# Twelve runs of unread products in the instruction stream of the matrix engine of a two-block transformer kernel

## The reference

```
# first model, layers 0 and 1
m = hybrid_mixer(x) if i == 0 else mla_mixer(x)     # recurrent + top-k attention; latent attention
h = layer_norm(ALPHA * x + m)
f = square(relu(h @ mlp_w1)) @ mlp_w2               # 1024 -> 4096 -> 1024
e = sigmoid(h @ ple_w_gate) * (p @ ple_w_proj)
x = layer_norm(ALPHA * h + f + e)
# second model, layers 0 and 1, on latent (512) and context (256) tokens
h = modulate(rms_norm(x), ...)                      # then ab_mixer (mLSTM + windowed attention) or c_mixer
x = x + gate * mixer(h)
x = x + gate * (square(relu(modulate(rms_norm(x)) @ w1)) @ w2)
```

## Time and profile before

| | us |
|---|---|
| three executions | 3631.1, 3635.57, 3611.84 (median 3631.1) |
| profiled execution, its own time | 3620.35 |
| span of its instructions | 3618.6 |
| PE busy | 3330.8 (92%) |
| PE weight loads busy | 2592.0 (72%) |
| DVE busy | 1654.2 (46%) |
| ACT busy | 1220.9 (34%) |
| POOL busy | 82.8 (2%) |
| mean granted clock of PE | 0.924 |

### The profile page before, as it was taken

How to read it: one execution, slowest core, us unless ns; L and a number is a source line. 1 busy time by engine, 2 the same in 40 slices (tenths; PEclk the granted TensorE clock), 3 DMA queues, 4 the chain that set the end, 5 groups by cost and what they waited for, 6 DMA issues and landing times. The chain is left out here.

```text
span 3618.6 us, 40069 instructions
## 1 busy us (share of the span) xinstructions
PE 3330.8 (92%) x15236; PEld 2592.0 (72%) x15236; DVE 1654.2 (46%) x2745; ACT 1220.9 (34%) x2016; POOL 82.8 (2%) x88
## 2 busy tenths in 40 slices
PE   7899999999999999999985998899999988989999
PEld 6576677763576677767864876778888865767777
DVE  3753566651253566653235565332332334343334
ACT  2343233322463233334121333232222233543332
POOL 4000000000000000000000010000000000000000
PEclk9859999999999999998985785999999989999999
DMA  4201434422301433421210000111111111012221
GB/s 153 71 1 53 150 130 155 162 96 35 82 1 53 169 133 134 162 81 47 62 50 1 1 1 1 47 47 70 52 64 70 46 47 47 1 47 93 93 93 70
DMA packets 160797, 259.40 MB, mean 72 GB/s; under 512 B 58476, under 2 KB 73194, under 8 KB 160556
## 3 DMA queue, kind: packets, MB, share of 16 engines
q1 hardware_dynamic: 158932, 252.94, 19.8%
q10 hardware_dynamic: 1628, 4.76, 0.3%
q0 software_dynamic: 128, 0.26, 0.0%
HBM read 255.85 MB, written 2.10 MB: 71 GB/s over the span
## 5 line engine op out<-in xcount | busy, mean ns | idle before, releaser
L1104 ACT ACTIVATE w_hi<-wbuf 128x1024 fp32r<-128x1024 f32 x330 | 348.9, 1060 | 1324.7 <-PE psA L726 1275.2
L724 PE MATMUL psA<-act_hi,w_hi 128*128 128x512 f32 (+1 forms) x1824 | 699.7, 384 | 62.6 <-DVE act_lo L1682 43.1
L725 PE MATMUL psA<-act_lo,w_hi 128*128 128x512 f32 (+1 forms) x1824 | 684.6, 375 | 0.0
L726 PE MATMUL psA<-act_hi,w_lo 128*128 128x512 f32 (+1 forms) x1824 | 683.9, 375 | 0.0
L1676 DVE TENSOR_TENSOR w_lo<-wbuf,w_hi 128x1024 fp32r<-128x1024 f32 x330 | 404.0, 1227 | 562.7 <-ACT w_hi L1104 555.1
L724 PE MATMUL psA<-hid_hi,w_hi 128*128 128x512 f32 (+1 forms) x1280 | 480.3, 375 | 34.3 <-ACT work L1104 30.9
L725 PE MATMUL psA<-hid_lo,w_hi 128*128 128x512 f32 (+1 forms) x1280 | 472.0, 369 | 0.0
L726 PE MATMUL psA<-hid_hi,w_lo 128*128 128x512 f32 (+1 forms) x1280 | 471.7, 369 | 0.0
L724 PEld LDWEIGHTS psA<-act_hi,w_hi 128*128 128x128 f32 x1824 | 349.8, 192 | 148.1 <-issue 52.6
L725 PEld LDWEIGHTS psA<-act_lo,w_hi 128*128 128x128 f32 x1824 | 350.9, 192 | 60.0 <-issue 3.6
L726 PEld LDWEIGHTS psA<-act_hi,w_lo 128*128 128x128 f32 x1824 | 349.9, 192 | 61.3
(11 more groups left out here) (214 smaller groups left out, 3750.2 us busy)
## 6 DMA issues: line engine op xcount, KB each, us to landing
wbuf<-in_mlp_w_dram SPq DMA_DIRECT2D x64, 2048.0 KB, 7.9
work<-in_ada_w_dram SPq DMA_DIRECT2D x32, 1536.0 KB, 12.3
wbuf<-in_ab_w_in_dram SPq DMA_DIRECT2D x10, 1024.0 KB, 5.0
wbuf<-in_ple_w_gate_dram SPq DMA_DIRECT2D x4, 2048.0 KB, 7.7
wbuf<-in_hy_w_in_dram SPq DMA_DIRECT2D x3, 2048.0 KB, 8.1
wbuf<-in_c_w_in_dram SPq DMA_DIRECT2D x3, 2048.0 KB, 7.5
wbuf<-in_hy_w_out_dram SPq DMA_DIRECT2D x2, 2048.0 KB, 8.0
wbuf<-in_mla_w_out_dram SPq DMA_DIRECT2D x2, 2048.0 KB, 7.8
```

Source lines behind the costliest of these rows:

```text
L724: pe.matmul(psA[:, s, a:b], w_hi, x_hi[:, a:b], start=first, stop=False)
L725: pe.matmul(psA[:, s, a:b], w_hi, x_lo[:, a:b], start=False, stop=False)
L726: ins = pe.matmul(psA[:, s, a:b], w_lo, x_hi[:, a:b], start=False, stop=last)
L1104: return nc.scalar.activation(out, in_, func, **kw)
```

## The change

A helper `keep_clock(out, n)` issues n plain f32 products of the constants: stationary `ident` (128x128), moving the first 512 columns of the constants' tile, into a PSUM bank that holds nothing at that moment. Nobody waits for them and nobody reads the bank. Twelve calls are put into PE's stream, with 126 products in all. Three stand before a `meet` (10, 13, 13), one after `mla_skv` (9), the others between a norm's sums and the stage behind it.

```diff
+            def keep_clock(out, n):
+                for _ in range(n):
+                    pe.matmul(out, ident, const[:, 0:512], start=True, stop=True)
...
             meet(pe)
             attention_ahead("dsa")
+            keep_clock(psO[:, 512:1024], 10)
             meet(pe)
             split_linear("hy_out", sH[LAT], sL[LAT], LAT, split_here("hy_out"), behind=mean_of("hy_out"))
             layer_norm(0, xT)
+            keep_clock(psO[:, 512:1024], 9)
             ple(0)
+            keep_clock(psO[:, 512:1024], 13)
             meet(pe)
             mlp("mlp0", 0, LAT)
             meet(pe)
             layer_norm(1, acc)
+            keep_clock(psO[:, 512:1024], 6)
...
             product("mla_skv", 0, [(0, LAT, [(C["mean"], rt[:, k, :]) for k in range(2)])])
+            keep_clock(psO[:, 512:1024], 9)
             for c in range(4):
                 w = weights(pe, "uq", c)
...
             layer_norm(2, xT)
+            keep_clock(psO[:, 512:1024], 9)
             ple(1)
+            keep_clock(psO[:, 512:1024], 13)
             meet(pe)
             mlp("mlp1", 1, LAT)
             meet(pe)
             layer_norm(3, acc)
+            keep_clock(psO[:, 512:1024], 7)
             rms(0, TOK)
+            keep_clock(psO[:, 512:1024], 13)
             split_linear("ab", abH, abL, TOK, split_here("ab"), AB_UNITS)
...
             split_linear("ab_out", sH[TOK], sL[TOK], TOK, split_here("ab_out"), behind=mean_square_of(1, TOK))
+            keep_clock(psB[:, 1, :], 13)
             mlp("mlp2", 2, TOK)
             rms(2, TOK)
+            keep_clock(psO[:, 512:1024], 13)
             split_linear("c_k", sH[TOK], sL[TOK], TOK, split_here("cin"), 2)
...
             split_linear("c_out", sH[LAT], sL[LAT], LAT, split_here("c_out"), behind=mean_square_of(3, LAT))
+            keep_clock(psO[:, 512:1024], 11)
             mlp("mlp3", 3, LAT)
```

## The result

The changed kernel takes 3649.77 us (median of 18 executions, 3639.11 to 3664.66), the kernel before 3618.56 (18 executions): ratio 1.0085, 95% interval 1.0068 to 1.0102. It is slower by 31 us, 0.85%, less than the one per cent that I set for "no change", but clear of the noise. I had said 3653, from +21.7 against 3631.1, the median of the first three executions; against the median of all 18 it would have been 3640. One of those 18 executions took 5499.74 us and one of `only_norms` 4826.73, far above all the others; the ratios leave both out, and without it the median of before is 3617.24.

The account below looks back on a forecast made before the run. PE sets the time, losing it in waits and at half clock. Place terms (filler overrun less clock gain) sum to +21.7 us on the 3631.1 median: 3653 us, range 3630 to 3672.

Parts of the forecast that it names:

- The mechanism: At each filler place: time by which filler outlasts the wait, less what the higher clock gives back; sum +21.7 us.
- The three sharpest terms: Net losses before the barriers of mlp0 and mlp1 and after mla_skv: +3.0, +3.5 and +7.7 us.
- the MLP barriers: Before mlp0 and mlp1, 13 products each: filler outlasts the wait, clock gives part back, net +3.0 and +3.5 us.
- +7.7 after mla_skv: Nine products where PE has no wait go straight onto its path: +7.7 us.
- the price of 0.86 a product: Every filler product is two records of 0.43 us at full clock, so 0.86 us.
- The pacing: Behind norms of 512 tokens ACT and DVE pace the first unit, hiding filler and cold time: 0, bounds ±1 each.
- The attention's barrier: Ten products before the barrier behind the first attention delay the work behind it: +11 us, bounds +9 and +13.
- the filler begins cold, ten products take 10.8: At the first attention's barrier: filler starts at half clock, ten products take 10.8 us, overrun +10.1.
- The wide norms: Three norms of 768 tokens, 13 products each: cold time after the last k saved, -3 us together, bounds -4.4 and +2.
- two of three hold: At the norms of 768 tokens, the clock stays up after the filler in two of three places: -3 us.
- The rival of one record per product: Every filler product costs one record, 0.43 us, so the change gives -2, 3629 us, not slower; chance 0.06.
- Absorption in uq and ukv: Rival: PE's later waits for ACT in uq and ukv absorb the mla_skv delay: +14, 3645 us; chance 0.12.

Follow-up runs that it names:

- only_norms: Changed kernel with only the eight filler calls in the waits of norms: 3631.86 us against 3631.13 before, ratio 1.0010.
- double_mlp: Changed kernel with 26 instead of 13 filler products before each of the barriers of mlp0 and mlp1: 3660.03 us, one execution.
- half_columns: Changed kernel with filler products of 256 columns instead of 512, same count: 3637.41 us, one execution.
- lean: `paced_fit` without the filler behind the norms of 512 tokens and before mlp2: 3626.14 us against 3635.03 before, ratio 0.9968.
- only_four: Changed kernel with only the four filler calls outside norms (three before barriers, one after mla_skv): 3640.85 us against 3631.13 before, ratio 1.0062.
- paced_fit: Changed kernel, filler cut to the waits, single products between ab's and c_k's waits, four behind the first attention's barrier: 3608.23 us against 3616.18 before, ratio 0.9981.
- dsa_twice: Kernel before, without filler, each logits product of the first attention issued twice: 3649.97 us, one execution.
- dsa_hold: `paced_fit` plus 11 filler products at waits just ahead of and in the first attention: 3598.81 us against 3635.03 before, ratio 0.9898.

## Why the prediction was right, point by point

- **The mechanism held.** The filler's overrun is lost in full, and what a higher clock gives back is the cold time that lay on PE's path. At a barrier both show: PE started 5.7 us later and at full clock, and the net is +3.2. The three sharpest terms came out to a tenth or two: +3.0 and +3.5 at the MLP barriers were +3.2 and +3.6, +7.7 after mla_skv was +7.7. `double_mlp` and `half_columns` confirm the price of 0.86 a product.
- **The pacing held.** Zero behind the 512-token norms, in both directions: adding filler (`only_norms`: +0.1, -0.1, 0.0) and leaving it out (`lean`: 0.0) moved nothing.
- **The attention's barrier was over-sized**, +11 against +8.5 (+7.9 in `only_four`, with a row of its own). The step was "the filler begins cold, ten products take 10.8". The clock rose at 258.7 in that trace, 1 us after the filler's start, so ten products took 9.1, and ACT's first work was 8.3 us late, not 10.1. In `only_four` it rose with the filler's first product. The rest behind it (4.31 us) and the cold stretch after it (272.3 to 275.7, 3.4 us) were as long as forecast, but cost 0.2 us more than before, not 0.9.
- **The wide norms were mis-sized**, -3 for the three against +1.6 (ab +1.4, mlp2 and c_k +0.2 together; rms(0) by itself was +0.3, forecast +0.2). The step was "two of three hold". None held: the clock fell again in the thin part in each (at 1675, 2402 and 2976), twice with a longer cold stretch behind the last k than before (5.7 and 3.3 us against 2.5 and 2.9). The row that I had seen, a rise and a fall in the middle of such a stretch, should have set the value, not half of it.
- **The rival of one record per product** fell with two records each, 0.43 us apart. (Its threshold of 0.44 a product is where the overrun begins; with 2.7 us given back by the clock, the loss begins near 0.64.) **Absorption in uq and ukv** fell with +7.7 at 881.7, and +7.7 still there at 945. **The clock not held** fell too: every filler ran at full clock or came to it within 1 us. By the Trainium skill (TensorE: Matmul & The Clock Gate, Part 4) transposes don't engage the upper level. No run here has a stretch of transposes alone, so none can settle it. What the kernel before shows is that turns (PE's transposes) among other products don't bring the clock down by themselves: its latent attention, with 157 turns among 660 records, is at 1.00 for 110 us (first line: the stretch; then two groups of its records, the 64-column products and the turns).

```profile
955.00:1065.00 110.00, 107.03 (x660) 84.07 (x658) 58.52 (x146) 67.90 (x194) 0.00 (x0) 1.00 0.13 45
L836 PE MATMUL psO<-work 128*128 128x64 f32 x312 | 42.5, 268 | 0.0
L687 PE MATMUL psB<-const,work 128*128 128x128 f32 x157 | 27.8, 276 | 2.1 <-ACT work L1104 2.0
```

- **The remainder.** Ratio 1.0085 is 31 us, the places give 24. The shares of the two groups don't explain the other 7: 10 of 17 executions of before lie in the lower one and 10 of 18 of after, with one more between the groups. The upper groups differ by the 24 of the places, the lower ones by 28, and the difference of the medians is larger still because both medians lie at the upper edge of the lower group; the cause of the extra 4 to 7 us stays open.
- **Luck in the number.** That it came out so near (3653 against 3649.77) owes some 12 us to the median of three executions that I added to. With the median of all 18 the same sum gives 3640, 9.5 us short. Within the sum, +11 for the attention's barrier was 2.5 too high and the wide norms 4.6 too low, which partly cancel.

## What to carry to other kernels

A filler is an order, not a hint: on an engine that executes in order it delays everything behind it, and ahead of a barrier it delays every other engine too. Size it to end before the wait does, put it behind the barrier, and only where the cold time that follows lies on the path; a unit that is paced by another engine hides cold time for nothing. Look for a wait at the head of a long stretch that is busy and still at half clock: eleven products there (19.7 us) brought more than all the rest of the filler (13.7 us of steps in `paced_fit`).

## What the runs showed of the hardware

- The same kind of work can run long at either level: the first attention ran 71 us at 0.50 after one wait of 3.4 us (`paced_fit`), and 48 us at 1.00 with that wait filled and single filler products ahead of it (`dsa_hold`); the latent attention, 110 us at 1.00.
- A busy PE is no sign of a high clock (97% in `paced_fit`, 69.26 of 71.2 us, and 99% in the kernel before, both at 0.50), and doubling the logits products didn't bring it back (`dsa_twice`, 33.7 us lost).
- One untouched stretch of 1259 records took 281, 295, 298, 311 and 315 us in the traces of different kernels, with mean clocks from 0.72 down to 0.61. That is enough to make the kernel's two groups of times, 21 us apart.
